# The gather of routed token rows: the third token tile padded from 32 to 128 partitions

## What is computed

```python
def moe_swiglu(x, w_router, wg, wu, wd):
    """Top-2-of-8 routing per token (softmax over the two selected logits)."""
    xf = x.reshape(-1, D_MODEL)
    logits = xf.astype(jnp.float32) @ w_router.astype(jnp.float32)
    vals, idx = lax.top_k(logits, TOP_K)
    wts = jax.nn.softmax(vals, axis=-1)
    gates = jnp.sum(jax.nn.one_hot(idx, N_EXPERTS, dtype=jnp.float32) * wts[..., None], axis=1)
    out = jnp.zeros(xf.shape, jnp.float32)
    for e in range(N_EXPERTS):
        out = out + gates[:, e:e + 1] * swiglu(xf, wg[e], wu[e], wd[e]).astype(jnp.float32)
    return out.astype(x.dtype).reshape(x.shape)
```

## Time and profile before

| | us |
|---|---|
| median of 3 runs | 1660.03 |
| lowest and highest run | 1659.11, 1660.29 |
| span of the profiled execution | 1658.4 |
| PE busy | 1580.2 (95% of the span) |
| DVE busy | 1192.4 (72%) |
| ACT busy | 961.0 (58%) |
| POOL busy | 56.3 (3%) |

### The profile page before, as it was taken

How to read it: one execution, slowest core, us unless ns; L and a number is a source line. 1 busy time by engine, 2 the same in 40 slices (tenths; PEclk the granted TensorE clock), 3 DMA queues, 4 the chain that set the end, 5 groups by cost and what they waited for, 6 DMA issues and landing times.

```text
span 1658.4 us, 22346 instructions
## 1 busy us (share of the span) xinstructions
PE 1580.2 (95%) x8017; PEld 1306.1 (79%) x8017; DVE 1192.4 (72%) x1088; ACT 961.0 (58%) x932; POOL 56.3 (3%) x90
## 2 busy tenths in 40 slices
PE   4899899999799699999999999999999999999996
PEld 3687699999687478878888888887887887887885
DVE  3635455544545468879879879879878887987886
ACT  4534444334335357757766766766766775776674
POOL 2010000000210100000000000000000000000001
PEclk9999899999799779999999999999999999999999
DMA  8433254440524059979979978979997997997992
GB/s 326 148 127 118 86 183 172 159 172 29 229 105 165 0 218 367 370 274 351 370 280 346 364 298 334 365 292 339 365 356 273 365 366 280 349 365 283 349 365 107
DMA packets 60618, 431.69 MB, mean 260 GB/s; under 512 B 6913, under 2 KB 7327, under 8 KB 8975
## 3 DMA queue, kind: packets, MB, share of 16 engines
q1 hardware_dynamic: 59966, 429.53, 68.6%
q0 software_dynamic: 608, 1.56, 0.3%
HBM read 428.60 MB, written 2.74 MB: 260 GB/s over the span
## 4 chain that ended last, share of the span: by engine, by line
PE 92%; DVE 4%; ACT 2%; issue 1%; POOL 1%; DMA 0%; POOLq 0%; DVEq 0%; SPq 0%; ACTq 0%
PE bank L265 28%; PE bank L267 27%; PE bank L266 27%; PE bank L1437 4%; PE bank L1461 1%; PE bank L1111 1%; DVE wlo L253 1%; ACT whi L249 1%; PE bank L1481 1%; ACT junk L438 1%; PE bank L1483 1%; DVE hT_lo L700 0%; ACT hT_hi L447 0%; DVE xn L693 0%; PE bank L1238 0%
## 5 line engine op out<-in xcount | busy, mean ns | idle before, releaser
L253 DVE TENSOR_TENSOR wlo<-raw,whi 128x2048 fp32r<-128x2048 f32 x402 | 920.5, 2291 | 209.2 <-ACT whi L249 208.9
L249 ACT ACTIVATE whi<-raw 128x2048 fp32r<-128x2048 f32 x402 | 769.0, 1915 | 189.7 <-PE bank L267 189.3
L265 PE MATMUL bank<-whi,gT_hi 128*128 128x512 f32 x896 | 365.1, 408 | 0.0
L267 PE MATMUL bank<-whi,gT_lo 128*128 128x512 f32 x896 | 355.4, 397 | 0.0
L266 PE MATMUL bank<-wlo,gT_hi 128*128 128x512 f32 x896 | 354.1, 395 | 0.0
L267 PEld LDWEIGHTS bank<-whi,gT_lo 128*128 128x128 f32 x896 | 169.2, 189 | 39.3
L265 PEld LDWEIGHTS bank<-whi,gT_hi 128*128 128x128 f32 x896 | 169.9, 190 | 36.0
L266 PEld LDWEIGHTS bank<-wlo,gT_hi 128*128 128x128 f32 x896 | 169.9, 190 | 34.8
L265 PE MATMUL bank<-whi,eT_hi 128*128 128x512 f32 x448 | 177.4, 396 | 1.0 <-DVE eT_lo L991 1.0
L266 PE MATMUL bank<-wlo,eT_hi 128*128 128x512 f32 x448 | 177.2, 396 | 0.0
L267 PE MATMUL bank<-whi,eT_lo 128*128 128x512 f32 x448 | 176.3, 393 | 0.0
(11 more groups left out here) (187 smaller groups left out, 1632.6 us busy)
## 6 DMA issues: line engine op xcount, KB each, us to landing
raw<-in_stream SPq DMA_DIRECT2D x402, 1024.0 KB, 4.8
table<-in_table SPq DMA_DIRECT2D x2, 896.0 KB, 14.4
const<-in_const SPq DMA_DIRECT2D x1, 1192.0 KB, 21.8
stage<-in_mem SPq DMA_DIRECT2D x2, 512.0 KB, 5.1
x<-in_x_prompt SPq DMA_DIRECT2D x1, 1024.0 KB, 11.2
out_y_prompt<-xm SPq DMA_DIRECT2D x2, 512.0 KB, 2.6
out_mem_k<-kv POOLq DMA_DIRECT2D x2, 256.0 KB, 4.3
out_mem_v<-kv POOLq DMA_DIRECT2D x2, 256.0 KB, 4.3
```

Of the source, the lines that this page charges most:

```text
L249: nc.scalar.activation(whi[:, slot % SPL, :], raw[:, slot, :], ACT.Copy).then_inc(hi_ready, 1)
L253: nc.vector.tensor_tensor(wlo[:, slot % SPL, :], raw[:, slot, :], whi[:, slot % SPL, :].bitcast(F), ALU.subtract).then_inc(lo_ready, 1)
L265: nc.tensor.matmul(out, a_hi, b_hi, start=start, stop=False, **kw)
L267: return nc.tensor.matmul(out, a_lo, b_hi, start=False, stop=stop, **kw)
```

## The change

The third token tile is treated as one of 128 rows in the gather. DVE zeroes `xm[:, 2, :]` once (128 x 1024), behind `gather_rows(0)`; `gather_rows(2)` later writes its first 32 partitions. `select` compares all 128 partitions of the third tile, where `posm` in partitions 32 to 127 is far negative, so `sel` is zero there. `gather` takes all 128 rows for each tile. The number and order of PE's instructions are the same; DVE has one instruction more. `turn_sel` and `scatter` stay as they are.

```diff
@@ -895,6 +895,7 @@
             dve.wait_ge(gain_in, 16)
             gather_rows(0)
+            V.memset(xm[:, 2, :], 0.0)
             dve.wait_ge(S["logit_turned"], 1)
@@ -966,9 +967,7 @@
                 def select(e):
 
                     for t in range(3):
-                        rr = ROWS[t]
-                        last = V.tensor_scalar(sel[0:rr, t, :], slots[0:rr, :], posm[0:rr, t, bass.ds(e, 1)], None,
-                                               ALU.is_equal)
+                        last = V.tensor_scalar(sel[:, t, :], slots[:, :], posm[:, t, bass.ds(e, 1)], None, ALU.is_equal)
                     last.then_inc(S["sel_out"], 1)
@@ -1433,9 +1432,8 @@
                     for k in range(4 * b, 4 * b + 4):
                         for t in range(3):
-                            rr = ROWS[t]
-                            last = T.matmul(bank[b][:, (k % 4) * P:(k % 4 + 1) * P], xm[0:rr, t, k * P:(k + 1) * P],
-                                            sel[0:rr, t, :], start=t == 0, stop=t == 2)
+                            last = T.matmul(bank[b][:, (k % 4) * P:(k % 4 + 1) * P], xm[:, t, k * P:(k + 1) * P],
+                                            sel[:, t, :], start=t == 0, stop=t == 2)
                     last.then_inc(S["gat_done"], 1)
```

## The result

The changed kernel takes 1632.8 us, median of four runs from 1629.35 to 1633.76; the kernel before took 1659.6 in the same comparison. The ratio is 0.984, with a 95% interval of 0.9824 to 0.9856: 24 to 29 us faster. The profiled execution is the fastest of the four, 1629.35 us with a span of 1627.5. So the two traces differ by 30.9 us and the medians by 26.8, and part of what follows is about that difference.

What follows compares the result with a forecast made beforehand. The prediction took PE as the bound, with gaps at changes between 128-row and 32-row matmuls on the path. Saving 22 (warm calls) + 8.1 (first gather and stream) - 0.5 (memset) = 29.6 us takes 1660.0 to 1630.4, range 1628.0 to 1635.5.

Steps and rivals of the forecast that it cites:

- What bounds: In the experts PE's matmuls set the end; gaps between their starts at each change of form are on the path.
- The warm calls: Seven experts' gathers, 14 calls: first matmul to L266 falls from 4.45 to 2.87 us, 22 us saved.
- The followers: In the experts, DVE's `wlo` split and the transfers keep up at 342 GB/s, costing nothing.
- The first gather: Clock rises 4.9 us after its start; DVE's splits then bound it, `turn_sel` at about 587.0, 6.6 us saved.
- The stream behind it: Product stream behind the first gather: some 2 us less if the clock holds, nothing if it falls; 1.5 taken.
- The memset: 128x1024 on DVE's router chain, 1.1 us long, hidden by `mask`'s wait unless POOL is delayed; 0.5 us cost taken.
- The sum: Whole kernel: 22 + 8.1 - 0.5 = 29.6 us saved, median 1660.0 becomes 1630.4.
- A: Rival: the clock stays low in the first gather; 26.3 us saved, 1633.7 us; chance 0.28.
- B: Rival: the weight stream becomes the bound, seven gathers give nothing, PE waits for `wlo`; 1652.4 us; chance 0.06.
- C: Rival: in the changed gather, loads no longer run ahead of matmuls; slower, 1681 us; chance 0.02.
- D: Rival: the gather's gaps are not of the form, only the memset is left; 1660 to 1661 us; chance 0.04.

Runs made afterwards that it cites:

- experiment 7: Changed kernel with padded matmuls only in the 14 warm gather calls, 32 rows in the first two; 1636.5 us, ratio 0.9869.
- experiment 3: Changed kernel with the third tile padded to 64 rows instead of 128 in the gather's matmuls; 1659.7 us, ratio 1.001.
- experiment 5: Kernel before with the gather's loops exchanged, token tile outside and feature block inside, no padding, no memset; 1636.9 us, ratio 0.9861.
- experiment 2: Changed kernel with the third tile padded to 96 rows instead of 128 in the gather's matmuls; 1631.6 us, ratio 0.9837.
- experiment 6: Changed kernel with padded matmuls only in the first gather (two calls), 32 rows in the 14 warm calls; 1653.4 us, ratio 0.9959.
- experiment 8: Changed kernel with the memset moved ahead of DVE's wait for the router's product; 1631.1 us, ratio 0.9829.
- experiment 9: Changed kernel with the memset moved right ahead of `mask`, inside the stall; 1629.7 us, ratio 0.9817.
- experiment 1: The changed kernel run again unchanged, as a control; 1632.5 us, ratio 0.9844.
- experiment 11: Changed kernel with memset right ahead of `mask`, `turn_sel` on full rows, and first `gate_up` ahead of `turn_sel`; 1626.4 us, ratio 0.9799.

## Why the prediction was right, point by point

The forecast was 1630.4 in a range of 1628.0 to 1635.5, and 29.6 us saved; measured are 1632.8 and 26.8.

- **What bounds.** Right: gaps between PE's starts in the experts were on the path, and all of what went from them came off the time (13 calls, 19.9 us).
- **The warm calls, 22 us.** 14 x 1.54 = 21.6 by the trace, 2.91 us to L266 where 2.87 was predicted, and 22 us (19 to 24) as a time of its own in experiment 7. One reading in this term was wrong without harm: the 0.34 us from L265 to L266 were taken for the payment of a change of form, but in the changed kernel they are still 0.32 (697.68 to 698.00). Only the way from the first record to L266 as a whole can be compared. The place of the loss, which I took from the 128-to-32 step inside a sum, is shown by experiments 3 and 5, and the price per change is 0.19 us (half of the 0.38 in experiment 5). What I called the form is coarser than the number of rows: 96 and 128 are one (experiment 2).
- **The followers.** Right: no new wait in the experts, and 342 GB/s as worked out.
- **The first gather.** 6.5 us to `turn_sel` for 6.6 predicted. The cause was the one given, the clock's rise inside the gather, but 6.1 us after its start in the two traces of the changed kernel and 3.4 to 5.2 in the other seven, where 4.9 was taken. The bound was not quite the one given. In the changed kernel `turn_sel` comes 9.94 us after the start, where 9.8 was worked out from DVE's splits, but the chain that ended last goes through the gather itself and not through the splits:

```profile
575.87 8.54 PE bank L1435 x48
584.43 0.61 ACT gT_hi L601
585.06 0.70 DVE gT_lo L975
585.81 0.61 PE bank L1444 x3
```

In experiments 2, 6, 8 and 9, where the rise came 4.2 to 4.5 us after the start, DVE's splits are the bound, and it takes 9.7. So the late rise cost only 0.2 us because DVE's splits hid the rest; that the forecast came out to 0.1 us is in part luck.
- **The stream behind it.** Here the time was overrated. I left open whether the clock would hold through PE's wait, and took 1.5 of 2 us. In the profiled run it held, and 2.5 us were saved; in experiments 2, 6, 8 and 9 it fell again, and 0.9 to 1.0 was left. Why it holds in one and falls in another stays open.
- **The memset, taken as 0.5 us.** 0.8. The step that failed is "that wait hides the memset". I had seen that `mask` stood still until POOL's L421 ended, and did not ask which instruction would stand still if the chain came later: `nfirst` came under L421 instead, and all of the chain behind it lay after L421's end. The stall did not shrink by the length of the memset; it moved forward in the chain.
- **The sum.** For a run like that of experiment 2 the pieces are 20.0 for 13 warm calls, 0.6 for the last call and the end with its clock, 6.8 for the first gather, 1.0 behind it and -0.8 for the memset, 27.6 together. 26.8 are measured, with an interval of 24 to 29. The fall of the clock at the end, about 1 us, was in no term of the prediction. The rest lies within the spread of both kernels' runs: the kernel before ranged from 1654.6 to 1661.5 in 21 runs.
- **The rivals.** A (the clock stays low) fell: it rose inside in each of the nine traces with a gather of few or no changes. B (the stream of weights) fell by the waits and by experiment 7. C fell: all loads here are on all rows, and the pace is 0.112 us. The rule of the Trainium skill ("TensorE: Matmul & The Clock Gate", Part 3) that a load overlaps only into another row group doesn't hold for these matmuls; the same Part also lets a load run ahead into the background weight buffer, which the rival left out and which the trace doesn't contradict. D fell with the result.

## What to carry to other kernels

Where a loop has one short operand among full ones (here 32 rows among 128), look at the starts of its matmuls and not at PE's busy share. A change between 32-row matmuls and 128-row ones cost 0.19 us each time at 2.4 GHz, nearly two of these records; 64 rows lost as much per call. Padding to the class of the neighbours (96 rows were enough) costs nothing on PE, and putting the short ones in a row gets most of it without any zeros. Before an instruction is put under a stall, write down what it will push into the stall: in experiment 9 the same memset was free, a few instructions behind the place where it had cost 0.8 us.

## What the hardware showed that I had not expected

- A 96-row matmul between 128-row ones is free, a 64-row one costs as much as a 32-row one (2.59 and 4.12 us for the same 24 records).
- A small `tensor_scalar` of DVE (128x2 here, 128x8 in `mask`) that starts while POOL's `tensor_tensor` over 128x1024 runs is finished only behind it: 1.44 and 2.21 us for what takes 0.21 alone. One case is at the border: in the kernel before and in experiment 9 the second `nfirst` starts 0.03 to 0.04 us behind the recorded start of L421 and isn't held. POOL's records are rough at that scale. MAX8 and a 128x1024 memset beside it ran at their own length (0.29 and 0.91 us).
- The same float32 matmuls held the clock at 1.2 GHz for 15 us when there were gaps between them, and let it rise within 3.4 to 6.1 us when there were none. Behind such a gather PE waited for `gT_lo`. In six traces the wait was 1.52 to 2.50 us and the clock fell again behind it; in two (the changed kernel and experiment 1) it was 1.41 us and in experiment 11 1.10 us, and the clock held. An early rise ends the gather earlier and so makes the wait longer, which takes part of the gain back. Nine traces don't show that the length of the wait alone decides.
